# Hybrid encoder layer with expert-choice MoE: merging and routing put in one block, gated sums kept in PSUM, first up weights split earlier, top-k searched on half-length rows, first gather issued by the routing block

## The chip, the cores and the metric

One Trainium2 chip, one core. The time is device microseconds of one launch of the kernel. Three runs of the kernel before gave a median of 2004.21 us (2004.15 to 2004.9).

## The reference, cut to what matters

Two sequences (512 and 256 tokens) get 16 meta tokens in front, so that there are 528 and 272 rows, 800 together, of width 1024. One layer does a mixer (window attention and a long convolution, each gated) and then an expert-choice mixture of 16 experts:

```python
merged = sigmoid(g_a) * (a_out @ w_attn_up) + sigmoid(g_h) * (h_out @ w_hyena_up)
h = h + merged @ w_out
hn = rmsnorm(h)                                   # gain norm_ffn_g
aff = softmax(hn @ w_router)                      # over 16 experts
g, idx = top_k(aff.T, cap)                        # per sequence: 66 of 528, 34 of 272
ye = (silu(hn[idx] @ w_gate[e]) * (hn[idx] @ w_up[e])) @ w_down[e] * g
out = h with ye added at the rows idx, then the final rmsnorm
```

## The kernel before, in words

All matmuls with weights are done in three passes (`three_passes`, lines 242 to 246): both operands are split in a high part, rounded to a narrower format, and a low part, the rest; hi by hi, hi by lo and lo by hi are summed in PSUM. So each weight tile is copied by ScalarE (`..._hi`) and subtracted by VectorE or GpSimd (`..._lo`) before TensorE can use it.

The program is a row of stages. Each is a block with one program per engine, written out by hand, and `end_stage()` behind it clears the stage's semaphores and holds all engines at a barrier.

* `stage_mix`: input projection, attention.
* `stage_hyena` (line 1021 on): the long convolutions by Fourier matmuls. 16 turns (8 pieces of width by 2 orders) go through spectrum (`kf`), forward transform (`zt`, `fwd`), product with the spectrum (`mul` on VectorE, `comb` on GpSimd), turning (`yt`, `yhi` on ScalarE, `ylo` on VectorE) and the way back (`inv`, `gate`). `steps` sets the order on all engines. After the last spectrum matmul SyncE loads the first three up weights and the attention rows (lines 1493, 1495, 1173), stores the last convolution rows (`store_out`, line 1143), and waits until these stores have landed (line 1177).
* `stage_merge` (line 1523 on): 8 weight pieces of 256 columns, each `[128, 4, 256]`; even ones of `w_attn_up`, odd ones of `w_hyena_up`. ScalarE splits the 8 row tiles (`up_in_hi`, line 1557) and the weights (`wu_hi`, line 1554), VectorE makes `up_in_lo` (line 1583), GpSimd `wu_lo` (line 1608). For a pair of pieces TensorE fills 8 PSUM banks: 4 units (two column tiles m, two halves of the 800 rows) by 2 (attention, convolution). VectorE multiplies both by their gates into `gated_pair` (line 1593), adds them into `merged` (line 1599), ScalarE copies that to `merged_hi` (line 1571), VectorE subtracts for `merged_lo` (line 1601). There are 16 units in all. `w_out` is loaded meanwhile, but not split.
* `stage_route` (line 1677 on): ScalarE makes `wo_hi` (line 1784), VectorE and GpSimd `wo_lo` (lines 1814, 1773), by turns. Then seven token tiles: TensorE does `product(i, 0)` and `product(i, 1)` (24 matmuls each), VectorE adds the residual (line 1820), ScalarE squares, a row scale is made, VectorE writes the normalised row `ffn_normed` (line 1827), TensorE turns it (line 1735), both copy it to `ffn_turned`, and TensorE multiplies by the router (line 1746). Then softmax, a transpose of the affinities, and on VectorE the top-k: nine rounds of MAX8, FIND_INDEX8 and MATCH_REPLACE8 (lines 1852 to 1857) on rows of 528, one partition for each expert and sequence. The lists are transposed to slots (`slot_tok`, lines 1866 to 1869). Meanwhile the first expert weights are loaded into the six-deep `w_ring`, and GpSimd splits four halves of them (`we_lo`, line 1777).
* `stage_experts` (line 1997 on): the first gather of rows by GpSimd (line 2000), after a copy of `slot_tok`, and then 16 experts of 12 weight chunks (2 MB each).

Where the order is by hand, a wait on one engine holds everything written behind it on that engine.

## Time and profile before

| what | us |
|---|---|
| median of three runs | 2004.21 |
| the profiled execution, its own time | 2004.04 |
| its span | 2002.2 |
| last row of the convolutions gated | 648.90 |
| first matmul of merging | 656.23 |
| last matmul of merging ends, about | 730.95 |
| first matmul of `product(0, 0)` | 744.95 |
| search of the top values, from and to | 853.75, 872.95 |
| first gather issued | 876.79 |
| first expert matmul | 884.76 |

Busy shares over the whole span: TensorE 93%, VectorE 71%, ScalarE 60%, GpSimd 17%. These are means over stages with different limits, so stages are read one by one below. In the rows, a time is the start in us from the span's start, the next number is the duration, and `[0.56 <-POOL wu_lo L1608]` is the idle time of the engine before the row and what ended it. PE is TensorE, DVE VectorE, ACT ScalarE, POOL GpSimd, SPq SyncE issuing DMAs.

### The profile page before, as it was taken

The numbers are of one execution on the slowest core, as the hardware profiler recorded it, in microseconds if no ns is written. First come the engines' busy times: TensorE is split into PE (matmuls) and PEld (weight loads), VectorE is DVE, ScalarE is ACT, GpSimd is POOL, SyncE is SP. The second block draws the span as 40 slices with busy tenths as digits, with TensorE's granted clock in tenths as the row PEclk, the third lists the DMA queues.
The fourth block names the chain that finished last, engine by engine and source line by source line (L and its number), as shares of the span: only waits on it lengthen the run. The fifth ranks groups of instructions, "written<-read, shape, count | busy, mean of one in ns | idle before, by whom it ended". The sixth has DMA issues, their size and how long they took to land.

```text
span 2002.2 us, 25117 instructions
## 1 busy us (share of the span) xinstructions
PE 1859.7 (93%) x9286; PEld 1449.9 (72%) x9286; DVE 1424.9 (71%) x1431; ACT 1200.3 (60%) x1323; POOL 333.2 (17%) x220
## 2 busy tenths in 40 slices
PE   5999999969998869839999999999999999999996
PEld 5989777848887868627777777777777777777774
DVE  4564211127665662369999999999999999999996
ACT  4225665634433321237777777777777777777776
POOL 1224111135542230040110000011001100010010
PEclk9999999979999889969999999999999999999998
DMA  5332121155012734269999999999999999999994
GB/s 186 105 86 81 54 86 65 40 159 135 23 50 82 254 121 179 103 215 369 361 373 393 376 375 379 388 377 371 383 381 380 372 390 371 374 379 388 377 355 184
DMA packets 239240, 506.51 MB, mean 253 GB/s; under 512 B 20929, under 2 KB 55593, under 8 KB 239112
## 3 DMA queue, kind: packets, MB, share of 16 engines
q1 hardware_dynamic: 228488, 484.63, 66.8%
q0 software_dynamic: 10688, 21.03, 4.4%
q8 instruction: 39, 0.64, 0.1%
q14 instruction: 25, 0.20, 0.0%
HBM read 474.64 MB, written 31.41 MB: 253 GB/s over the span
## 4 chain that ended last, share of the span: by engine, by line
PE 54%; DVE 0%; ACT 0%; issue 0%; DMA 0%; POOL 0%; POOLq 0%; DVEq 0%; ACTq 0%
PE bank L244 18%; PE bank L246 18%; PE bank L245 18%; PE bank L2032 2%; DMA gathered<-ffn_rows,slots_next 0%; ACT we_hi L2090 0%; DVE we_lo L2165 0%; POOL out L2023 0%; DVE w_ring L2246 0%; ACT L2106 0%; DVE expert_out L2230 0%; DVE w_ring L2251 0%; ACT w_ring L2150 0%; DVE hidden L2187 0%; DVE gate_silu L2183 0%
## 5 line engine op out<-in xcount | busy, mean ns | idle before, releaser
L2165 DVE TENSOR_TENSOR we_lo<-w_ring,we_hi 128x2048 fp32r<-128x2048 f32 x380 | 860.6, 2288 | 78.0 <-ACT we_hi L2090 73.3
L2090 ACT ACTIVATE we_hi<-w_ring 128x2048 fp32r<-128x2048 f32 x380 | 724.4, 1914 | 97.6 <-PE bank L246 97.4
L244 PE MATMUL bank<-we_hi,gathered_turned_hi 128*100 128x512 f32 x1024 | 406.9, 397 | 1.4 <-DVE gathered_turned_lo L2169 1.4
L246 PE MATMUL bank<-we_hi,gathered_turned_lo 128*100 128x512 f32 x1024 | 403.2, 394 | 0.0
L245 PE MATMUL bank<-we_lo,gathered_turned_hi 128*100 128x512 f32 x1024 | 402.5, 393 | 0.0
L246 PEld LDWEIGHTS bank<-we_hi,gathered_turned_lo 128*100 128x100 f32 x1024 | 168.5, 165 | 69.6
L244 PEld LDWEIGHTS bank<-we_hi,gathered_turned_hi 128*100 128x100 f32 x1024 | 168.8, 165 | 65.7 <-issue 1.7
L245 PEld LDWEIGHTS bank<-we_lo,gathered_turned_hi 128*100 128x100 f32 x1024 | 168.5, 165 | 65.2
L244 PE MATMUL bank<-normed_hi,w_hi 128*128 128x400 f32 x544 | 199.3, 366 | 11.4 <-ACT gate_sig L635 6.9
L244 PE MATMUL bank<-we_hi,hidden_turned_hi 128*100 128x512 f32 x512 | 204.2, 399 | 0.0
L245 PE MATMUL bank<-we_lo,hidden_turned_hi 128*100 128x512 f32 x512 | 201.6, 394 | 0.0
L246 PE MATMUL bank<-we_hi,hidden_turned_lo 128*100 128x512 f32 x512 | 201.3, 393 | 0.0
L245 PE MATMUL bank<-normed_lo,w_hi 128*128 128x400 f32 x544 | 190.2, 350 | 0.0
L246 PE MATMUL bank<-normed_hi,w_lo 128*128 128x400 f32 x544 | 190.0, 349 | 0.0
L2010 POOL DMA_INDIRECT residual_rows<-expert_out,slots_now x15 | 42.1, 2808 | 840.9 <-DVE expert_out L2199 840.9
L244 PEld LDWEIGHTS bank<-normed_hi,w_hi 128*128 128x128 f32 x544 | 104.8, 193 | 32.5 <-issue 18.2
L852 POOL TENSOR_TENSOR w_lo<-w_raw,w_hi 128x2048 fp32r<-128x2048 f32 x17 | 79.0, 4649 | 273.3 <-ACT w_hi L595 273.3
L246 PEld LDWEIGHTS bank<-we_hi,hidden_turned_lo 128*100 128x100 f32 x512 | 84.3, 165 | 34.0
L244 PEld LDWEIGHTS bank<-we_hi,hidden_turned_hi 128*100 128x100 f32 x512 | 84.4, 165 | 31.3
L245 PEld LDWEIGHTS bank<-we_lo,hidden_turned_hi 128*100 128x100 f32 x512 | 84.5, 165 | 31.0
L245 PEld LDWEIGHTS bank<-normed_lo,w_hi 128*128 128x128 f32 x544 | 104.6, 192 | 0.1
L246 PEld LDWEIGHTS bank<-normed_hi,w_lo 128*128 128x128 f32 x544 | 104.4, 192 | 0.1
(296 smaller groups left out, 2619.3 us busy)
## 6 DMA issues: line engine op xcount, KB each, us to landing
w_ring<-in_w_exp_gate SPq DMA_DIRECT2D x64, 2048.0 KB, 14.0
w_ring<-in_w_exp_up SPq DMA_DIRECT2D x64, 2048.0 KB, 13.7
w_ring<-in_w_exp_down SPq DMA_DIRECT2D x64, 2048.0 KB, 15.5
w_raw<-in_w_in SPq DMA_DIRECT2D x68, 256.0 KB, 4.2
gate_rows<-gate_sig SPq DMA_DIRECT2D x16, 400.0 KB, 2.5
sig_pair<-gate_rows SPq DMA_DIRECT2D x8, 800.0 KB, 5.0
hy_conv_rows<-u_conv SPq DMA_DIRECT2D x12, 400.5 KB, 3.1
w_out<-in_w_out SPq DMA_DIRECT2D x8, 512.0 KB, 7.6
```

Source lines behind the costliest of these rows:

```text
L244: nc.tensor.matmul(out, whi, xhi, start=first, stop=False)
L245: nc.tensor.matmul(out, whi, xlo, start=False, stop=False)
L246: return nc.tensor.matmul(out, wlo, xhi, start=False, stop=last)
L852: nc.gpsimd.tensor_tensor(wlo[c % 2][:, :, :], raw[c % 3][:, :, :], whi[c % 2][:, :, :].bitcast(F32), ALU.subtract).then_inc(w_lo, 1)
L2010: pool.indirect_dma_start(g.accS[:, :], bass.IndirectOffsetOnAxis(ap=cur[0:SLOTS, 0:1], axis=0), ye[0:SLOTS, :], None, compute_op=ALU.add) ...
L2032: last = nc.tensor.transpose(tb[n % 2][:, k * P:k * P + SLOTS], src, ident[0:SLOTS, 0:SLOTS])
L2090: act.activation(whi[(2 * k + half) % 4][:, :], ring[k % RING][:, half * HC:(half + 1) * HC], ACT.Copy).then_inc(w_hi, 1)
L2165: nc.vector.tensor_tensor(wlo[u][:, :], ring[k % RING][:, half * HC:(half + 1) * HC], whi[u][:, :].bitcast(F32), ALU.subtract).then_inc(w_ ...
```

## The change

* `stage_merge` is gone; its work is the first part of `stage_route`, in the same block, with no barrier between.
* Up weights 0 and 1 are split at the end of the convolution block: `wu_hi` on ScalarE behind the last `zhi` step, `wu_lo` on GpSimd at its end. `wu_lo` now lies over the raw weights (in place), so the load of piece i waits until TensorE is done with piece i - 4.
* SyncE's wait for the last stores is moved from the end of the convolution block to the start of the next one.
* For the first pair of pieces TensorE goes by row tile k first and unit second; before it went unit by unit.
* The gated sum stays in the PSUM bank of the convolution half; `merged` and the second half of `gated_pair` are gone. The convolution matmuls of the next pair wait for `m_lo`.
* `w_out` is split during merging: `wo_hi` on ScalarE behind sums 5 to 12, all of `wo_lo` on GpSimd between the up weights.
* TensorE turns the residual row itself, not the normalised one: the gain is multiplied into the router weights (`wrg`, eight more small loads for `gcol`), the row scale into the logits. Sums of squares are taken by halves.
* The top-k rows are halved: the long sequence of each expert lies in two partitions (256 and 272 entries), the short one in a third. Slot j takes the larger of the first list's j-th and the second list's (65 - j)-th.
* GpSimd issues the first gather in the routing block, straight from `slot_tok`. GpSimd's four `we_lo` go to VectorE: two behind `slot_tok`, two in the expert block. One chunk less is loaded ahead.

```diff
@@ stage_hyena, GpSimd, at its end
+            for i in range(2):
+                pool.wait_ge(g.wu_hi_done, i + 1)
+                nc.gpsimd.tensor_tensor(g.wu_lo[i][:, :, :], g.up_w[i][:, :, :], g.wu_hi[i][:, :, :].bitcast(F32), ALU.subtract)\
+                  .then_inc(g.wu_lo_done, 1)
@@ stage_hyena, SyncE, at its end
-            for k in range(4):
-                sp.wait_ge(store[k], 32)
@@ stage_hyena, ScalarE
+                if st == ("zhi", len(TURNS) - 1):
+                    act.wait_ge(kmm, before[len(TURNS)])
+                    for i in range(2):
+                        act.wait_ge(g.up_w_in[i], 32 if i % 2 == 0 else 16)
+                        act.activation(g.wu_hi[i][:, :, :], g.up_w[i][:, :, :], ACT.Copy).then_inc(g.wu_hi_done, 1)
@@ merging, VectorE, one unit
-                    for q in range(2):
-                        last = nc.vector.tensor_tensor(ga[:, q, :], banks[u % 4][q][:, 0:HALF], sig[m % 2][:, q, h * HALF:(h + 1) * HALF],
-                                                       ALU.mult)
-                    last.then_inc(gd, 1)
+                    nc.vector.tensor_tensor(ga[:, :], part[0], gate[0], ALU.mult)
+                    nc.vector.tensor_tensor(part[1], part[1], gate[1], ALU.mult).then_inc(gd, 1)
                     dve.wait_ge(gd, u + 1)
-                    nc.vector.tensor_tensor(mm_[:, :], ga[:, 0, :], ga[:, 1, :], ALU.add).then_inc(summed, 1)
+                    nc.vector.tensor_tensor(part[1], part[1], ga[:, :], ALU.add).then_inc(summed, 1)
@@ merging, ScalarE
+                    if 2 <= m < 6:
+                        out_weights(2 * (m - 2) + b)
@@ merging, TensorE
+                order = [(k, u) for k in range(GROUP) for u in range(4)] if c == 0 else [(k, u) for u in range(4) for k in range(GROUP)]
+                for k, u in order:
+                    if c and k == 0:
+                        pe.wait_ge(m_lo if q else gd, 4 * (c - 1) + u + 1)
@@ routing, TensorE
+                if i < 2 and b == 0:
+                    pe.wait_ge(m_lo, 2 * KT - 3 + i)
...
                     if i == 0 and b == 0:
-                        pe.wait_ge(w_lo[k % 2], k // 2 + 1)
+                        pe.wait_ge(o_lo, k + 1)
+                        pe.wait_ge(m_lo, 2 * k + 1)
...
-                pe.wait_ge(hnd, i + 1)
...
+                    if k % 4 == 0:
+                        pe.wait_ge(h2d, 2 * i + k // 4 + 1)
+                    last = nc.tensor.transpose(g.ps[4 + k // 4][:, (k % 4) * P:(k % 4) * P + m], h[i % 2][0:m, k * P:(k + 1) * P],
                                                ident[0:m, 0:m])
@@ routing, GpSimd
+            pool.wait_ge(slots, 2)
...
+            nc.gpsimd.indirect_dma_start(g.xe[0:SLOTS, :], None, g.hnS[:, :], bass.IndirectOffsetOnAxis(ap=g.slot_tok[0:SLOTS, 0:1], axis=0))\
+              .then_inc(g.gath, 16)
@@ routing, VectorE, at its end
+            for u in range(2):
+                dve.wait_ge(g.ew_hi_done, u + 1)
+                nc.vector.tensor_tensor(g.ew_lo[u][:, :], g.ring[u // 2][:, u % 2 * HC:(u % 2 + 1) * HC], g.ew_hi[u][:, :].bitcast(F32),
+                                        ALU.subtract).then_inc(g.ew_lo_done, 1)
```

Three places where the order on an engine moves. First ScalarE (ACT) at the end of the convolution block. `y_turned` is the turned spectrum that the last two ways back need. Before:

```order
L1344 ACTIVATE z_turned_hi_3802<-bank 128x256
L1346 ACTIVATE z_turned_rest_3774<-bank 16x128
L1347 ACTIVATE z_turned_rest_3774<-bank 16x128
L1358 ACTIVATE y_turned_hi_3811<-bank 128x512
L1364 ACTIVATE y_turned_rest_3813<-bank 32x128
L1365 ACTIVATE y_turned_rest_3813<-bank 32x128
L1358 ACTIVATE y_turned_hi_3811<-bank 128x512
```

and now:

```order
L1347 ACTIVATE z_turned_hi_3809<-bank 128x256
L1349 ACTIVATE z_turned_rest_3781<-bank 16x128
L1350 ACTIVATE z_turned_rest_3781<-bank 16x128
L1373 ACTIVATE wu_hi_3748<-up_weights_3740 128x1024
L1373 ACTIVATE wu_hi_3749<-up_weights_3741 128x1024
L1361 ACTIVATE y_turned_hi_3818<-bank 128x512
L1367 ACTIVATE y_turned_rest_3820<-bank 32x128
```

The two copies, and the waits for their loads, stand ahead of the turning of the last two turns.

Second TensorE (PE) between merging and routing. Before, two branches and the barrier stand between the last up matmul and the first of `product(0, 0)`:

```order
L244 MATMUL bank<-up_in_hi_6986,wu_hi_6989 128x400
L245 MATMUL bank<-up_in_lo_6987,wu_hi_6989 128x400
L246 MATMUL bank<-up_in_hi_6986,wu_lo_6991 128x400
L1523 UNCONDITIONAL_BRANCH
L1714 UNCONDITIONAL_BRANCH
L244 MATMUL bank<-wo_hi_7740,merged_hi_6984 128x512
```

and now:

```order
L244 MATMUL bank<-up_in_hi_6998,wu_hi_3749 128x400
L245 MATMUL bank<-up_in_lo_6999,wu_hi_3749 128x400
L246 MATMUL bank<-up_in_hi_6998,wu_lo_3747 128x400
L244 MATMUL bank<-wo_hi_7004,merged_hi_6996 128x512
L245 MATMUL bank<-wo_lo_7000,merged_hi_6996 128x512
```

The products follow at once.

Third GpSimd (POOL) from merging to the first gather. Before:

```order
L1608 TENSOR_TENSOR wu_lo_6991<-up_weights_3743,wu_hi_6989 128x1024
L1523 UNCONDITIONAL_BRANCH
L226 ISA
L1769 UNCONDITIONAL_BRANCH
L1773 TENSOR_TENSOR wo_lo_7741<-w_out_3739,wo_hi_7740 128x1024 x4
L1777 TENSOR_TENSOR we_lo_3754<-w_ring_66_3744,we_hi_3750 128x2048
```

and now:

```order
L1814 TENSOR_TENSOR wu_lo_3746<-up_weights_3742,wu_hi_3748 128x1024
L1819 TENSOR_TENSOR wo_lo_7000<-w_out_3739,wo_hi_7004 128x1024 x2
L1814 TENSOR_TENSOR wu_lo_3747<-up_weights_3743,wu_hi_3749 128x1024
L1819 TENSOR_TENSOR wo_lo_7000<-w_out_3739,wo_hi_7004 128x1024 x2
L1826 DMA gathered_3764<-ffn_rows,slot_tokens_52 100x1024
```

All eight `wo_lo` are on GpSimd now, within merging, no `we_lo` is, and the gather stands in this block.

## Rows read from the trace of the kernel before

**Rows 1.** Windows: us; busy us (instructions) of PE, PEld, DVE, ACT, POOL; granted clock; DMA share; GB/s
```profile
685.40:703.70 18.30, 17.74 (x97) 17.44 (x97) 10.22 (x16) 4.05 (x6) 4.79 (x2) 1.00 0.48 164
730.95:744.95 14.00, 0.00 (x0) 0.00 (x0) 11.02 (x14) 8.75 (x10) 7.47 (x3) 0.68 0.47 153
744.95:758.69 13.74, 13.74 (x50) 11.03 (x51) 5.87 (x2) 0.00 (x0) 4.79 (x2) 0.82 0.79 292
853.75:872.95 19.20, 0.00 (x0) 0.00 (x0) 18.61 (x43) 3.12 (x2) 15.81 (x4) 0.50 0.98 356
872.95:884.76 11.81, 2.00 (x11) 1.54 (x11) 2.79 (x21) 1.01 (x2) 1.09 (x1) 0.50 0.45 160
884.76:2002.20 1117.44, 1099.99 (x4984) 788.95 (x4984) 1019.69 (x700) 846.04 (x594) 83.91 (x33) 0.99 1.00 363
```

**Rows 2.** Timeline of ACT and DVE at the end of the convolutions
```profile
637.14 0.60 ACT L1358 ACTIVATE y_turned_hi<-bank 128x512 fp32r<-128x512 f32 x1 [2.66 <-PE bank L1276]
...
648.46 0.44 DVE L1466 TENSOR_TENSOR x_short<-bank,x_short 128x272 f32<-128x272 f32 x1 [3.49 <-PE bank L1291]
```

**Rows 3.** SyncE's issue of up weight 1; DMA issues (count, KB, us to landing), weights 0, 1
```profile
634.59 0.61 SPq L1495 DMA_DIRECT2D up_weights<-in_w_hyena_up  x1
...
up_weights<-in_w_attn_up SPq DMA_DIRECT2D x2, 256.0 KB, 4.1
...
up_weights<-in_w_hyena_up SPq DMA_DIRECT2D x1, 512.0 KB, 5.3
```

**Rows 4.** SyncE's wait for the last store; timeline of ACT, PE where merging starts
```profile
SPq L1177 <- DMA mixer_rows<-x_short: 1.3, 1, 1.3
...
651.88 0.87 ACT L1557 ACTIVATE up_in_hi<-attention_rows 128x800 fp32r<-128x800 f32 x1 [7.93 <-PEq L227]
...
659.83 0.87 ACT L1557 ACTIVATE up_in_hi<-hyena_rows 128x800 fp32r<-128x800 f32 x1 [3.85 <-DMA hyena_rows<-mixer_rows]
...
656.23 0.67 PE L244 MATMUL bank<-up_in_hi,wu_hi 128*128 128x400 f32 x1 [7.88 <-POOL wu_lo L1608]
```

**Rows 5.** Timeline of DVE and PE within merging
```profile
673.53 2.24 DVE L1599 TENSOR_TENSOR merged<-gated_pair 128x400 f32<-128x400 f32 x1
...
676.88 1.05 DVE L1593 TENSOR_TENSOR gated_pair<-bank,sig_pair 128x400 f32<-128x400 f32 x2
677.96 0.58 DVE L1599 TENSOR_TENSOR merged<-gated_pair 128x400 f32<-128x400 f32 x1
...
679.63 1.05 DVE L1593 TENSOR_TENSOR gated_pair<-bank,sig_pair 128x400 f32<-128x400 f32 x2
...
685.41 0.42 PE L244 MATMUL bank<-up_in_hi,wu_hi 128*128 128x400 f32 x1 [0.56 <-POOL wu_lo L1608]
```

**Rows 6.** Timeline of PE and DVE in routing: last tile, copies, first search
```profile
846.02 1.06 PE L1735 MATMUL bank<-ident,ffn_normed 32*128 32x32 f32 x8 [4.54 <-DVE ffn_normed L1827]
...
852.51 0.68 DVE L1846 COPY affinity<-bank 16x512 f32<-16x512 f32 x1 [1.74 <-PE bank L1762]
...
853.28 0.43 DVE L1848 COPY affinity<-bank 16x272 f32<-16x272 f32 x1
853.75 0.70 DVE L1852 MAX8 top_values<-affinity 48x8 f32<-48x528 f32 x1
```

**Rows 7.** Timeline of DVE, POOL: slot list, gathers; of the chain: first gather's landing
```profile
874.69 0.15 DVE L1869 TENSOR_TENSOR slot_tokens<-bank,second_group_slots 100x1 uint32<-100x1 f32 x1
...
876.79 1.09 POOL L2000 DMA_INDIRECT gathered<-ffn_rows,slots_next  x1 [7.23 <-DVE slots_next L2261]
...
876.79 4.95 DMA gathered<-ffn_rows,slots_next
...
1039.09 4.49 DVE L2165 TENSOR_TENSOR we_lo<-w_ring,we_hi 128x2048 fp32r<-128x2048 f32 x2 [0.29 <-ACT we_hi L2090]
...
1039.21 3.08 POOL L2000 DMA_INDIRECT gathered<-ffn_rows,slots_next  x1 [8.26 <-DMA residual_rows<-expert_out,slots_now]
...
1176.24 1.03 POOL L2000 DMA_INDIRECT gathered<-ffn_rows,slots_next  x1 [8.19 <-DMA residual_rows<-expert_out,slots_now]
```

More of the change, by code:

```diff
@@ L947, in stage_hyena @@
         S("hy_x2_long0 hy_x2_long1 hy_x2_short0 hy_x2_short1")
-    store = S("hy_store0 hy_store1 hy_store2 hy_store3")
+    store = g.hy_store
     steps = hyena_steps()
@@ L1506, in stage_merge @@
     ulo = sb("up_in_lo", [P, KT, T], F32R)
-    sb.at = g.merge_rest_at
-    whi = [sb("wu_hi", [P, GROUP, WCH], F32R) for _ in range(2)]
-    wlo = [sb("wu_lo", [P, GROUP, WCH], F32R) for _ in range(2)]
+    sb.at = g.up_rows_at
+    olo = sb("wo_lo", [P, KT, D], F32R)
+    whi, wlo = g.wu_hi, g.wu_lo
+    sb.at = g.merge_rest_at + 2 * GROUP * WCH * 4
     sig = [sb("sig_pair", [P, 2, T]) for _ in range(2)]
-    ga = sb("gated_pair", [P, 2, HALF])
-    mm_ = sb("merged", [P, HALF])
-    (up_in, u_hi, u_lo, wh, wl, sg0, sg1, prod, gd, summed, m_hi, m_lo) = S(
-        "mg_up_in mg_u_hi mg_u_lo mg_wh mg_wl mg_sg0 mg_sg1 mg_prod mg_gated mg_sum mg_m_hi mg_m_lo")
@@ L1515, in stage_merge @@
-    sgs = [sg0, sg1]
+    ga = sb("gated", [P, HALF])
+    sb.at = g.merge_rest_at + 2 * GROUP * WCH * 4 + 4 * T * 4 + 3 * HALF * 4
+    ohi = sb("wo_hi", [P, KT, D], F32R)
+    assert sb.at <= nc.sbuf_usable_end, sb.at
+    sb.at = g.merge_rest_at - 4 * GROUP * WCH * 4
+    h = [sb("residual_in", [P, D]) for _ in range(2)]
+    hn = [sb("ffn_normed", [P, D]) for _ in range(2)]
+    gain = sb("ffn_gain", [P, D])
+    hT = sb("ffn_turned", [P, KT, P])
+    wr = sb("w_router", [P, KT, E])
+    wrg = sb("w_router_gain", [P, KT, E])
@@ new lines, in stage_route @@
+    gcol = sb("ffn_gain_col", [P, KT])
+    ss = sb("square_sums", [P, 3, NTOK])
+    rs = sb("row_scale", [P, NTOK])
+    lg = sb("logits", [P, NTOK, E])
+    red = sb("softmax_cols", [P, 2, NTOK])
+    EE = 64 + E
+    ROWS = (slice(0, E), slice(32, 32 + E), slice(64, EE))
+    PART = 2 * P
+    WIDE = LENS[0] - PART
+    parts = sb("affinity_by_token", [P, NTOK, EE])
+    af = [sb(f"affinity{x}", [EE, WIDE]) for x in range(2)]
+    rounds = -(-CAPS[0] // 8)
+    val = sb("top_values", [EE, 8 * rounds])
@@ L1516, in stage_merge, with row_parts @@
+    hin, st, hst, sgs = [hin0, hin1], [st0, st1], [hst0, hst1], [sg0, sg1]
+    pieces = [token_pieces(t0, m, io["x_prompt"][0], io["x_sample"][0], io["meta_tokens"]) for t0, m in TOK_TILES]
+    total = [[0, 0]]
+    for i, ps_ in enumerate(pieces):
+        now = list(total[-1])
+        now[i % 2] += 16 * len(ps_)
+        total.append(now)
     banks = [(g.ps[0], g.ps[1]), (g.ps[2], g.ps[3]), (g.ps[4], g.ps[5]), (g.ps[6], g.ps[7])]
-    NW = 2 * NCH
+    acc = banks[0:2]
     def up(k):
         return g.up_attn[:, k, :] if k < GROUP else g.up_hyena[:, k - GROUP, :]
+    def row_parts(k):
+        return [slice(0, HALF), slice(HALF, T)] if k == 0 else [slice(0, T)]
@@ L1529, in load_sig, with load @@
                 sp.dma_start(sig[m % 2][:, :, :], g.sigS.rearrange("(q m p) t -> m p q t", q=2, p=P)[m]).then_inc(sgs[m % 2], 16)
+            def load(i):
+                if i >= 2:
+                    sp.wait_ge(trn, i - 1)
+                    sp.wait_ge(hnd, i - 1)
+                    sp.wait_ge(hst[i % 2], 16 * (i // 2))
+                for r0, src in pieces[i]:
+                    sp.dma_start(h[i % 2][r0:r0 + src.shape[0], :], src).then_inc(hin[i % 2], 16)
+            for k in range(4):
+                sp.wait_ge(g.hy_store[k], 32)
             for k in range(GROUP, KT):
@@ L1686, in _ @@
+                    load_sig(2)
+                    load_sig(3)
+            for m in range(4, KT):
+                load_sig(m)
+            sp.wait_ge(upd, 4 * NW)
             load(0)
@@ L1874 @@
 RING = 6
-AHEAD = RING + 2
+AHEAD = RING + 1
 FCH = FE // 4
@@ L1915, in stage_experts @@
     ye = sb("expert_out", [P, D])
+    gain = sb("final_gain", [P, D])
+    first_rows = sb("first_rows", [P, D])
+    assert sb.at <= g.ew_lo_at, sb.at
+    sb.at = g.ex_small
     nxt = sb("slots_next", [P, 1], U32)
@@ L1926, in stage_experts @@
     row_of = [sb("out_row", [P, 1], U32) for _ in range(2)]
-    gain = sb("final_gain", [P, D])
-    first_rows = sb("first_rows", [P, D])
+    assert sb.at <= g.up_rows_at, sb.at
     def ring_part(k, i):
@@ L2269, in _ @@
                 turn_lo(c, "x", c)
+            for half in range(2):
+                lo_of(0, 1, half)
             nc.vector.memset(stat[:, :], 1.0).then_inc(fconst, 1)
```

493 lines of the change are left out of this document (237 added, 256 removed).

## The prediction

> **What bounds the kernel now.** I read the busy shares first, then the windows by stage, then the timelines at the seams, then the waits. The experts take 1117.44 us of the span [rows 1], and TensorE works in 1099.99 of them at granted clock 0.99, so nothing on VectorE, ScalarE or the queues has a price there as long as it keeps its lead. The change touches the 236 us between the end of the convolutions (648.90, the end of the gate in [rows 2]) and the first expert matmul (884.76). There TensorE is the bound within the stages: between 685.40 and 703.70 it works 17.74 of 18.30 us [rows 1]. What can be had lies at the seams, where it stands still: 656.23 - 648.90 = 7.3 us ahead of merging, 14.00 us between merging and routing [rows 1], and the tail from the last tile's turning (846.02 [rows 6]) to 884.76, a chain of short work on VectorE, 19.20 us of it the search [rows 1]. The measurement can tell about 0.2% from no change, 4 us.
>
> **The sum, part by part,** against the profiled execution's own 2004.04 us, which lies 0.17 under the median.
>
> *1. The two weight copies on ScalarE, +3.9.* They stand ahead of the turning of the last two turns, and wait for their loads. Weight 0 was issued just before 634.59 and took 4.1 us, weight 1 was issued at 634.59 and took 5.3 [rows 3]: it is there at 639.9. A copy of 512 columns takes 0.60 us [rows 2], of 800 0.87 [rows 4], so one of 1024 some 1.05. So ScalarE is free at 640.95, where it began `y_turned_hi` at 637.14 [rows 2], waiting only for TensorE: +3.8, and 0.1 for TensorE's clock, which may fall meanwhile. Queued behind it are the copies for the last two ways back; VectorE's low part and, behind that in its order, the last product with the spectrum wait too, then GpSimd's sum and TensorE's turning. Nothing of this chain has slack, so the block ends at 652.8, not 648.9. GpSimd's two `wu_lo` come behind its own last work and end before that. Bounds: 0 if the loads land 4 us sooner, +9 if they take 10 us.
>
> *2. The stores' wait, -1.4.* SyncE waited 1.3 us [rows 4] before the barrier could open; ScalarE began merging at 651.88 [rows 4], 3.0 us behind the gate. Now the queue's issue of the store and the barrier are left, some 1.6. The loads of the convolution rows still wait for the stores, so they move by the 3.9 less about 1: `hyena_rows` let ScalarE go on at 659.83 [rows 4], now at 662.6.
>
> *3. First up matmul, -3.2.* It came at 656.23, 4.35 us behind ScalarE's start, held by `wu_lo` [rows 4]. Now the weights are ready, and it waits for half a row tile on ScalarE and VectorE: 1.15 us. It starts at 655.4. By row tiles first, each tile gives TensorE 12 matmuls, 2.2 us or more, where VectorE needs 1.0; the first attention half lasts to 666.3, and the late convolution rows are split by 664.6. That cover is 1.7 us: if it goes, the late rows are paid one by one.
>
> *4. Within merging, -0.9.* Before, TensorE waited for `wu_lo` once a pair, 0.56 us idle [rows 5] and 0.7 with the slower restart, three times: 2.1. In the steady pairs this goes, since piece i is split a half pair earlier. But in the first pair all four units now end together, while VectorE takes 2.75 us for one (679.63 - 676.88 [rows 5]); the second pair waits for the gates of its third and fourth unit, 0.6 each: 1.2. The convolution half's wait for `m_lo` falls 6 us behind its need. A unit costs TensorE 4.4 us, so VectorE's 2.75 stay covered. That the sum of 2.24 us beside a GpSimd instruction goes [rows 5], 0.58 otherwise, saves nothing: it was covered. GpSimd takes 4.79 us for two `wu_lo` [rows 1], so six of them and eight `wo_lo` of the same size some 34 us in 60; ScalarE's eight copies fit too, and both are done before they are needed.
>
> *5. The seam, -14.0.* `product(0, 0)` needs the sum of its last tile only at its last k, 4.9 us in, and VectorE is 4.6 behind. All 14.00 us [rows 1] go. The first pair then comes without the spell of low clock: its 13.74 us at 0.82 [rows 1] are 11.27 at full, *-2.5*. The small loads (`gcol`) land about as the first product ends, and the turning that needs them is a product later: 0.
>
> *6. Last tile to the search, -1.8.* The last turning waited 4.54 us for the normalised row [rows 6]. Now it waits for the residual alone, but ScalarE's copy for the router matmul still stands behind its squares and root: I take 2.1 of the 4.54, less 0.3 for a clearing that the exponential waits for and for affinities in three pieces. Ends: 0 and -3.7.
>
> *7. Copies, search, lists, -6.15.* A VectorE copy costs (0.68 - 0.43) / 240 = 1.04 ns a column [rows 6]. 26 instructions (nine MAX8, nine FIND_INDEX8, eight MATCH_REPLACE8, 0.7 us each) shorten by 256 columns: 26 x 0.267 = -6.9, of 19.20. Copies shared with ScalarE: -0.35. Two more list pieces and a choice of five small instructions more: +1.1. Ends of the search: -5.5 if the fixed part weighs more, -7.5.
>
> *8. The gather, +0.2.* From the slot list (874.84 [rows 7]) to the gather's issue at 876.79 is 1.95 us, and it lands 4.95 later [rows 7], so 6.9. Now it is issued without the copy and the barrier, 0.7 behind the list. But VectorE starts `we_lo` at once. At 1039.21 a gather issued 0.12 us into a `we_lo` took 3.08 us, ending 0.9 behind the first of the two (4.49 / 2); at 1176.24 one took 1.03 [rows 7]. I take the former: it ends 3.25 us behind the list, lands 3.86 after that, 7.1: +0.2. The barrier, behind VectorE's 4.6 us, opens at 5.7 and is covered. If it isn't held: -1.0.
>
> The Trainium skill's page "SBUF — State Buffer" (section "Who interferes with whom") speaks against the value I take. It says that a `tensor_tensor` with both inputs in SBUF contends only with GpSimd's reads, and infers that writing descriptors isn't held by it. By that rule the gather goes ahead, the barrier becomes the later one, and the sum is about 1.2 us lower; the row of 3.08 us disagrees.
>
> *9. The experts, 0.* VectorE has two halves more to split, 4.5 us [rows 7], just behind the first turned rows; chunk 1 is needed one chunk later, 5.8 us (1117.44 / 192) or more at the low clock. One chunk less is loaded ahead; chunk 7 is issued some 5 us into the experts and needed five chunks in, at 29. The engine that bounds this stage does the same work.
>
> Sum: 3.9 - 1.4 - 3.2 - 0.9 - 14.0 - 2.5 - 1.8 - 6.15 + 0.2 = -25.85, so 1978.2 us, 1.3% less. **Forecast: 1978.**
>
> **The rivals.**
> *A. The seam stays in part.* GpSimd is late with `wo_lo`: its eight wait for ScalarE's copies, these for the sums, and then each row tile of the first product is paced by 2.4 us or more, not 0.7. For: before, four of them took GpSimd 7.47 + 4.79 us beside VectorE [rows 1]. Against: VectorE's instructions in merging now read at most one SBUF operand, and the last sum that a copy waits for is the twelfth of 16. If four were left, 10 us come back: 1988.
> *B. ScalarE's stall is dear.* The loads take 10 us instead of 5: +5, 1983. For: the four attention rows, 1.6 MB, are issued right behind them. Against: they were before too, when the rows of 4.1 and 5.3 us were taken [rows 3].
> *C. Slower than before.* The mechanism: PSUM as source and target of VectorE's gate and sum. If each of these two instructions costs what the sum cost when it was blocked, 2.24 instead of 0.58 [rows 5], a unit takes 2.75 + 2 x 1.67 = 6.1 us, over TensorE's 4.4. From 4.4 on it decides, 16 units by 1.7 us are 27, and the time is 2005 to 2009. Against: no row here reads or writes PSUM on VectorE at such a price; the gates already read it, at 0.53 each.
> *D. The waits are replaced and nothing moves*: the tail's gain is lost to the gather, and the seam's to `m_lo`. 2000 to 2006. I see no row for it.
>
> **Chances.** Forecast with its unknown costs (1972 to 1984): 0.80. A: 0.06. B: 0.08. C: 0.03. D: 0.03. What is under 1972 lies in the first. The unknown costs: part 1 from -3.9 to +5 against my value, part 6 from -1.9 to +1.8, part 7 from -0.6 to +1.4, part 8 -1.2, an earlier return of the clock at the start -2, stalls in merging up to +3. Not all fall on one side; I reach from 1971 to 1985. Faster by over 0.2% (under 2000) in the forecast, A and B, and a little of D: 0.95. Within: 0.02. Slower: 0.03.
>
> **What would show it.** In the new profile: ScalarE idle some 5 us ahead of `wu_hi`, released by the up weights' load, and the last gate near 652.8; TensorE's first up matmul near 655.4; one or two waits of 0.6 us at the second pair and none later; `product(0, 0)` right behind the last up matmul, near 728 to 729; FIND_INDEX8 at 0.43; the gather of 3 us on GpSimd from the slot list on, and the first expert matmul near 859; then 1117 us of experts. The prediction falls if TensorE stands still between merging and routing, if a unit on VectorE takes over 4.4 us, or if the experts' stretch is longer by more than 2 us.

## The result, and the profile after

The changed kernel took 1984.04 us in the median of four runs (1982.3 to 1984.68), the kernel before 2004.18 on the same chip: a ratio of 0.9906, 95% interval 0.9893 to 0.9919. So it is 0.9% faster, 20 us, where the forecast said 26 and 1978. 0.9906 of 2004.21 is 1985.4, just outside the range that ended at 1985; the median itself, 1984.04, is at its edge. The profiled execution took 1984.68 us, its span 1982.9.

Read in the forecast's own order. First the windows by stage of the changed kernel (us; busy us (instructions) of PE, PEld, DVE, ACT, POOL; granted clock; DMA share; GB/s): merging, first product pair, search, slot list to first expert matmul, experts.

```profile
656.18:729.22 73.04, 72.37 (x385) 71.31 (x386) 37.74 (x66) 25.79 (x35) 33.36 (x14) 0.98 0.59 206
729.22:740.30 11.08, 11.08 (x49) 9.01 (x49) 5.49 (x13) 1.01 (x2) 0.00 (x0) 1.00 0.66 183
832.84:845.19 12.35, 0.00 (x0) 0.00 (x0) 11.77 (x43) 6.87 (x4) 0.00 (x0) 0.50 1.04 389
848.43:866.14 17.71, 1.57 (x8) 1.29 (x9) 5.92 (x9) 1.01 (x2) 5.04 (x1) 0.50 0.47 142
866.14:1982.90 1116.76, 1099.04 (x4984) 788.41 (x4984) 1023.78 (x705) 846.04 (x594) 75.97 (x33) 0.99 1.00 365
```

They answer to [rows 1]. The granted clock is a share of full speed. The stop of 14.00 us between merging and routing is gone: merging ends and routing begins within one row, and the first pair runs at full clock in 11.08 us instead of 13.74. The search fell from 19.20 to 12.35. The experts are as long as before, 1116.76 for 1117.44. One window went the other way: from slot list to first expert matmul it was 884.76 - 874.84 = 9.92 us, and is 17.71.

ScalarE at the end of the convolutions, timeline, beside [rows 2]:

```profile
639.39 1.06 ACT L1373 ACTIVATE wu_hi<-up_weights 128x1024 fp32r<-128x1024 f32 x1 [3.63 <-DMA up_weights<-in_w_attn_up]
641.33 1.06 ACT L1373 ACTIVATE wu_hi<-up_weights 128x1024 fp32r<-128x1024 f32 x1 [0.88 <-DMA up_weights<-in_w_hyena_up]
642.29 0.58 ACT L1361 ACTIVATE y_turned_hi<-bank 128x512 fp32r<-128x512 f32 x1
...
648.86 0.60 ACT L1361 ACTIVATE y_turned_hi<-bank 128x512 fp32r<-128x512 f32 x1 [5.56 <-PE bank L1279]
...
654.89 3.24 ACT L1655 ACTIVATE up_in_hi<-attention_rows 128x400 fp32r<-128x400 f32 x5 [5.02 <-PEq L227]
```

Both copies wait for their loads, and `y_turned_hi` stands behind them. TensorE in merging and at the seam, timeline, beside [rows 4, 5]:

```profile
656.18 0.67 PE L244 MATMUL bank<-up_in_hi,wu_hi 128*128 128x400 f32 x1 [3.31 <-DVE up_in_lo L1707]
...
680.53 0.45 PE L244 MATMUL bank<-up_in_hi,wu_hi 128*128 128x400 f32 x1 [0.28 <-DVE bank L1719]
683.26 0.45 PE L244 MATMUL bank<-up_in_hi,wu_hi 128*128 128x400 f32 x1 [0.26 <-DVE bank L1719]
...
729.03 0.34 PE L246 MATMUL bank<-up_in_hi,wu_lo 128*128 128x400 f32 x1
729.22 0.39 PE L244 MATMUL bank<-wo_hi,merged_hi 128*128 128x512 f32 x1
```

TensorE waits three times in all. The last row is `product(0, 0)`, directly behind the last up matmul. VectorE beside it, one unit with PSUM as source and target:

```profile
676.69 0.56 DVE L1718 TENSOR_TENSOR gated<-bank,sig_pair 128x400 f32<-128x400 f32 x1
677.17 0.57 DVE L1719 TENSOR_TENSOR bank<-bank,sig_pair 128x400 f32<-128x400 f32 x1
677.77 0.58 DVE L1721 TENSOR_TENSOR bank<-bank,gated 128x400 f32<-128x400 f32 x1
678.93 0.58 DVE L1723 TENSOR_TENSOR merged_lo<-bank,merged_hi 128x400 fp32r<-128x400 f32 x1 [0.57 <-ACT merged_hi L1674]
679.42 0.56 DVE L1718 TENSOR_TENSOR gated<-bank,sig_pair 128x400 f32<-128x400 f32 x1
```

A unit takes 679.42 - 676.69 = 2.73 us. The place that decided, all engines' timelines from the slot list on, beside [rows 7]:

```profile
848.28 0.15 DVE L1804 TENSOR_TENSOR slot_tokens<-pick 100x1 uint32<-100x1 f32 x1
848.34 4.49 DVE L1807 TENSOR_TENSOR we_lo<-w_ring,we_hi 128x2048 fp32r<-128x2048 f32 x2
848.75 5.04 POOL L1826 DMA_INDIRECT gathered<-ffn_rows,slot_tokens  x1 [126.53 <-DVE slot_tokens L1804]
852.86 0.37 SPq L1933 DMA_DIRECT2D w_ring<-in_w_exp_gate  x1
863.20 1.57 PE L2074 MATMUL bank<-ident,gathered 100*128 100x100 f32 x8 [16.17 <-PEq L227]
866.14 0.74 PE L244 MATMUL bank<-we_hi,gathered_turned_hi 128*100 128x512 f32 x1 [1.38 <-DVE gathered_turned_lo L2211]
```

The DMA issues of that stretch (us from issue to landing), and the block's last instruction on GpSimd's queue (duration ns min/median/max, first and last start):

```profile
w_ring<-in_w_exp_gate SPq DMA_DIRECT2D x1, 2048.0 KB, 10.5
gathered<-ffn_rows,slot_tokens POOLq DMA_INDIRECT x1, 13.4
```

```profile
L1581 POOLq DRAIN  x1: 13767/13767/13767, 848.5 to 848.5; - x1
```

The 17.71 us are now a plain sum. GpSimd begins 0.32 us behind the slot list. The issue takes 5.04 us and ends at 853.79, 0.96 behind the second `we_lo` (848.34 + 4.49 = 852.83). Weight chunk 6, 2 MB, is issued at 852.86, 0.9 us ahead of that end, and the gather's data land at 848.75 + 13.4 = 862.15. GpSimd's drain, the end of its block, lasts to 862.27, so the barrier opens only behind the landing and TensorE turns the first rows at 863.20. 0.32 + 13.4 + 1.05 + 2.94 = 17.71.

### The profile page after: what moved, and what is told of

Read it like the earlier page. It is cut to its first block, busy times and chain, and to the rows that moved or that the text cites. A ratio compares the mean times of both kernels' runs of the same rounds, so it can differ in the third digit from the quotient of the medians.

```text
span 1982.9 us, 25130 instructions
## 1 busy us (share of the span) xinstructions
PE 1855.6 (94%) x9286; PEld 1445.9 (73%) x9286; DVE 1409.5 (71%) x1447; ACT 1202.1 (61%) x1340; POOL 318.1 (16%) x220
## 4 chain that ended last, share of the span: by engine, by line
PE 54%; DVE 1%; issue 0%; ACT 0%; POOL 0%; POOLq 0%; DVEq 0%; ACTq 0%
PE bank L245 18%; PE bank L244 17%; PE bank L246 17%; PE bank L2074 2%; DVE we_lo L2207 1%; DVE w_ring L2272 0%; ACT we_hi L2132 0%; POOL out L2065 0%; DVE w_ring L2288 0%; ACT L2148 0%; DVE expert_out L2272 0%; DVE w_ring L2293 0%; ACT w_ring L2192 0%; DVE gate_silu L2225 0%; ACT gate_sigmoid L2148 0%
## 6 DMA issues: line engine op xcount, KB each, us to landing
w_ring<-in_w_exp_up SPq DMA_DIRECT2D x64, 2048.0 KB, 14.7
```

## The experiments

The profiled executions differ by some us ahead of anything that the change touches: ScalarE's last copy of the spectra begins at 633.03 before, at 634.31 after, and between 628.95 and 633.95 in the runs below. So "from the spectra" counts from there: before, the last gate ends after 15.87 us, the first up matmul comes after 23.20, the first product after 111.92, the search after 220.72, and the slot list is done after 241.81. "List to expert" is from the slot list's end to the first expert matmul. Ratios are against the kernel before on the same chip, with 95% intervals; they are 2.6 to 3.8 us wide to either side of the value, so smaller differences of the kernel's time are not told apart by them. The stretches of one profile each agree far better where the code is the same (MAX8 to the slot list: 15.58 to 15.60 us in every profile with the narrow search), so the parts are read from stretches.

**The changed kernel once more**, on another chip.

> The changed kernel itself, unaltered, on the same chip as the kernels beside it, as their measure. Expected: 1984 within 1.5 us; from ScalarE's last copy of the spectra to the last gate of the convolutions 19.1 to 20.1 us, to the first up matmul 21.9 to 22.8, from the slot list's end to the first expert matmul 17.7.

Measured: 1986.9 us, 0.9919 (0.9903 to 0.9935). Last gate after 20.04, first up matmul 22.80, first product 96.71, search 200.37, slot list 215.96; list to expert 17.51. The stretches agree with the first profile within 1.9 us, and the one at the gather within 0.2.

**What the loss at the gather consists of.** The first edit takes chunk 6 out of the routing block:

```diff
-AHEAD = RING + 1
+AHEAD = RING
```

> Only the seventh weight chunk's load is taken out of the routing block (it is issued first thing in the experts). Theory: the 17.7 us from slot list to first expert matmul are GpSimd's issue held by VectorE's two low parts (5.0 us), then the gather's data behind the 2 MB chunk, then GpSimd's drain until it has landed. Without the chunk ahead the gather lands some 4 to 5 us behind the issue's end instead of 8.4, and the first expert matmul comes 3.5 to 4.5 us sooner: about 1980. Rival 1, the chunk is no matter and the hold alone delays: no change, 1984. Rival 2, the block's end itself (drain, clearing, barrier) is long whatever the gather does: no change, and the drain does not end with the landing. If the chunk is late in the experts instead, the experts' stretch of 1116.8 us grows by what was won.

Measured: 1981.91 us, 0.9887 (0.987 to 0.9903). List to expert 13.55 us, 4.2 less than 17.71. The issue was held just as long, the landing came sooner, and the drain shrank with it (timeline of GpSimd; DMA issues; GpSimd's drain):

```profile
850.15 5.05 POOL L1826 DMA_INDIRECT gathered<-ffn_rows,slot_tokens  x1 [126.55 <-DVE slot_tokens L1804]
```

```profile
gathered<-ffn_rows,slot_tokens POOLq DMA_INDIRECT x1, 9.2
```

```profile
L1581 POOLq DRAIN  x1: 9598/9598/9598, 849.9 to 849.9; - x1
```

So the 2 MB ahead of the gather's data cost it 4.2 us, and both rivals fall: the chunk does matter, and the block's end is long only because of the gather. The experts took 1117.93 us, for 1116.76 and 1118.73 in the two profiles of the changed kernel; the later chunk cost nothing that can be seen.

The second moves the two low parts to GpSimd, ahead of the slot list. That is where they stood before the change, with two more, four in the time of a search of 19.20 us:

```diff
         def _(pool):
+            for u in range(2):
+                pool.wait_ge(g.ew_hi_done, u + 1)
+                nc.gpsimd.tensor_tensor(g.ew_lo[u]...)        # taken out of VectorE's program
             pool.wait_ge(slots, 2)
```

> The two low parts of the first expert weights are moved from VectorE, behind the slot list, to GpSimd, ahead of it in the time of the search. Theory: GpSimd's issue of the gather is then not held (1.0 to 1.1 us instead of 5.0), and chunk 6, whose load waits for the low parts, has landed before: the gather lands 4 to 5 us behind its issue, the drain ends with it, and the first expert matmul comes some 9.5 us behind the slot list instead of 17.7: 8 us less, about 1976. Rival 1 (block end long by itself): under 1 us less. Rival 2 (GpSimd beside the search slows VectorE): the search of 12.35 us grows by up to 2 us, and 6 us are left of the 8.

Measured: 1975.34 us, 0.9853 (0.9837 to 0.987). List to expert 10.01 us, 7.7 less. GpSimd's timeline, the DMA issues, the drain:

```profile
829.77 9.09 POOL L1818 TENSOR_TENSOR we_lo<-w_ring,we_hi 128x2048 fp32r<-128x2048 f32 x2 [112.19 <-ACT we_hi L1700]
844.13 1.09 POOL L1826 DMA_INDIRECT gathered<-ffn_rows,slot_tokens  x1 [5.27 <-DVE slot_tokens L1804]
```

```profile
gathered<-ffn_rows,slot_tokens POOLq DMA_INDIRECT x1, 5.7
```

```profile
L1581 POOLq DRAIN  x1: 6057/6057/6057, 843.9 to 843.9; - x1
```

The issue takes 1.09 us, the data land 5.7 behind its start, and MAX8 to the slot list takes 15.59 us as in the changed kernel, with GpSimd's 9.09 us beside it: both rivals fall. Hold (5.04 - 1.09 = 3.95) and chunk (4.2) make 8.15, and 7.7 came back: the data landed 4.6 us behind the issue's end, where it was 4.15 in the kernel without chunk 6. The experts took 1120.46 us in this profile, the longest of all sixteen (the others 1115.7 to 1118.7), so this profile alone doesn't show that the whole gain is kept; the three kernels further down with the same edit took 1115.7 to 1118.1 there.

**What holds the issue.** In two kernels the subtractions are replaced by instructions of another kind on the same tiles, so that the first chunk's low part is left out (lines shortened):

```diff
-                nc.vector.tensor_tensor(g.ew_lo[u], ring_half, g.ew_hi[u], ALU.subtract)
+                nc.vector.tensor_copy(g.ew_lo[u], ring_half)                          # one kernel
+                nc.vector.tensor_reduce(g.ew_lo[u], ring_half.unsqueeze(2), AX.X, ALU.max)   # the other
```

> VectorE's two low parts behind the slot list are replaced by copies of the weights (one input from SBUF instead of two); this leaves out the subtraction for the first chunk's low part. Theory: GpSimd's issue of the gather is held because VectorE reads two inputs from SBUF; with one input it is not held, and takes 1.0 to 1.1 us instead of 5.0, although VectorE is busy. Rival 1, any long VectorE instruction on SBUF holds it: it ends some 0.9 us behind the end of the first or second copy. Rival 2, the hold is not VectorE's but the queue's or the stores': 5 us as before.

> VectorE's two low parts behind the slot list are replaced by reductions over an axis of one element, which read one input from SBUF and run at one element a cycle; this leaves out the subtraction for the first chunk's low part. Theory: GpSimd's issue is not held by VectorE being busy as such, but by instructions that take the port the two share; the reduction does not, so the issue takes 1.0 to 1.1 us while VectorE works for 4 us beside it. Rival, every long VectorE instruction on SBUF holds it: the issue ends some 0.96 us behind the end of the first or second reduction.

Timelines of VectorE and GpSimd, first with copies:

```profile
847.35 2.35 DVE L1807 CAST we_lo<-w_ring 128x2048 fp32r<-128x2048 f32 x2
847.75 2.91 POOL L1825 DMA_INDIRECT gathered<-ffn_rows,slot_tokens  x1 [126.56 <-DVE slot_tokens L1804]
```

then with reductions:

```profile
846.84 4.47 DVE L1807 TENSOR_REDUCE we_lo<-w_ring 128x2048 fp32r<-128x2048 f32 x2
847.24 1.09 POOL L1825 DMA_INDIRECT gathered<-ffn_rows,slot_tokens  x1 [126.58 <-DVE slot_tokens L1804]
```

With the copies (1981.34 us in one run, list to expert 15.99) the issue ends at 850.66, 0.96 behind the second copy; my theory, that it takes two inputs from SBUF, falls, and its rival 1 came true. With reductions it takes 1.09 us inside 4.47 us of VectorE work, so it isn't VectorE's being busy either, and that rival falls as well. What holds it is a kind of instruction: subtractions with two inputs in SBUF and copies (2048 columns in 1.2 us, against 2.2 for either of the others). The gather then went ahead of chunk 6, landed after 5.2 us, and list to expert was 9.49 us (1974.44 in one run) with nothing moved to GpSimd.

Why to the end of the second? One low part of the two is moved:

```diff
-            for u in range(2):        # VectorE, behind the slot list
+            for u in range(1, 2):     # u = 0 is on GpSimd, ahead of the slot list
```

> The first of the two low parts is on GpSimd ahead of the gather, the second stays on VectorE behind the slot list. Theory: the issue is held while VectorE's low parts follow one another without a gap, to the end of the last: with one left it ends 0.96 us behind that one, some 2.8 us after its start instead of 5.04, and the first expert matmul comes about 2.2 us sooner behind the slot list, 15.5 us. Rival, the issue needs several turns of the port and takes one between the two: it would then take about as long, 3 us, but end at another place than 0.96 behind the low part.

Measured: 1978.1 us (one run); list to expert 15.45. VectorE and GpSimd:

```profile
844.28 2.29 DVE L1807 TENSOR_TENSOR we_lo<-w_ring,we_hi 128x2048 fp32r<-128x2048 f32 x1
844.68 2.84 POOL L1830 DMA_INDIRECT gathered<-ffn_rows,slot_tokens  x1 [9.71 <-DVE slot_tokens L1804]
```

The issue ends 0.95 us behind the one low part, where the theory put it. In seven profiles with two subtractions it ended 0.96 behind the second (and so with the two copies). But this is no rule, as the expert loop shows, where low parts also come in pairs without a gap. Of the 224 gathers there from `ffn_rows` (16 profiles), 150 began 0.055 us or more behind the start of a low part, and each ended 0.90 to 0.92 us behind the end of that same one, with the next instruction already under way. The other 74, begun at most 0.04 us behind its start, or ahead of it, took 1.03 us. Only the last gather of each profile, from `residual_rows`, was held to the end of the second, in all 16; in the kernel before (timelines of VectorE and GpSimd):

```profile
1929.29 4.48 DVE L2165 TENSOR_TENSOR we_lo<-w_ring,we_hi 128x2048 fp32r<-128x2048 f32 x2
1930.58 4.09 POOL L2000 DMA_INDIRECT gathered<-residual_rows,slots_next  x1 [8.46 <-DMA residual_rows<-expert_out,slots_now]
```

Why some gathers get in behind the first of two and others only behind the second was not tried. Chunk 6 was still ahead of it, issued at 846.59, and the gather landed 11.1 us behind its start.

**The gather back behind the barrier.**

```diff
         def _(pool):            # expert block
+            nc.gpsimd.indirect_dma_start(g.xe..., g.hnS..., slot_tok[0:SLOTS, 0:1])   # taken out of routing
             for e in range(E - 1):
```

> The first gather is issued behind the barrier again (from the slot list itself, without the copy of before); everything else as in the changed kernel, so VectorE's low parts and chunk 6 stay where they are. Theory: the barrier opens behind the low parts, some 1.1 us after 852.8, the issue takes 1.1 us, and chunk 6 is still ahead of the data, so the gather lands at about the same time as now (862 to 863.5); what goes is the drain and the barrier behind the landing, 1.0 us. First expert matmul 0 to 1 us sooner: 1983 to 1984. Rival, issuing in routing is worth what it was meant to be: 1 to 2 us slower than the changed kernel, 1985 to 1986. Rival, the drain costs much more than 1 us: 3 us or more less.

Measured: 1984.47 us, 0.9906 (0.989 to 0.9923): the changed kernel's ratio. List to expert 17.22 us. GpSimd's drain, then its timeline and TensorE's:

```profile
L1581 POOLq DRAIN  x1: 45/45/45, 847.6 to 847.6; - x1
```

```profile
854.25 1.09 POOL L2044 DMA_INDIRECT gathered<-ffn_rows,slot_tokens  x1 [133.14 <-issue]
861.59 1.60 PE L2074 MATMUL bank<-ident,gathered 100*128 100x100 f32 x8 [15.64 <-DMA gathered<-ffn_rows,slot_tokens]
```

Without a gather in flight the drain takes 45 ns. TensorE starts as soon as the rows are there, not 1.05 us later. Issuing it 6.6 us sooner, as the changed kernel does, made the first expert matmul 0.3 to 0.5 us later. Neither rival came true.

**The copies of the first up weights last on ScalarE.**

```diff
-                if st == ("zhi", len(TURNS) - 1):
+                if st == ("yhi", len(TURNS) - 1):
                     ...                               # the two wu_hi
```

> ScalarE's two copies of the first up weights stand behind its last turned rows in the long convolutions instead of ahead of the rows before. Theory (part 1 of the sum): the copies and the wait for their loads held the chain at the end of the convolutions by 3.9 us with the clock; that goes, and GpSimd's low parts end at about the block's end or 0.6 us behind: 3.0 to 3.9 us less, about 1980.5. Rival, the chain had slack or the clock's fall sets it: under 1 us less. Rival, the low part comes too late for the first up matmul: it waits for wu_lo again, and 1 us or less is left.

Measured: 1983.27 us, 0.9895 (0.9878 to 0.9911), which alone tells nothing. The stretches do: the last gate comes after 15.87 us, the very figure of before, where ten kernels with the copies ahead show 19.04 to 20.74, in the mean 19.8. ScalarE and GpSimd:

```profile
643.37 0.60 ACT L1361 ACTIVATE y_turned_hi<-bank 128x512 fp32r<-128x512 f32 x1 [4.77 <-PE bank L1279]
...
644.42 2.01 ACT L1373 ACTIVATE wu_hi<-up_weights 128x1024 fp32r<-128x1024 f32 x2
```

```profile
645.55 4.69 POOL L1104 TENSOR_TENSOR wu_lo<-up_weights,wu_hi 128x1024 fp32r<-128x1024 f32 x2 [1.89 <-ACT wu_hi L1373]
```

The first rival falls. Of the 3.9 us, 1.1 go to the wait for GpSimd's second low part (to 650.24, behind the gate's end at 649.34), and the first up matmul comes after 19.77 instead of 22.5 (mean of the ten): 2.8 us less.

**The first up weights split behind the barrier again.**

```diff
-        ...                           # the two wu_hi and two wu_lo in the convolutions' block
         act.wait_ge(g.up_attn_in, 16 * GROUP)
-        for k in range(GROUP):
+        weights(0)
+        rows(0)
+        weights(1)
+        for k in range(1, GROUP):
             rows(k)
...
-        for i in range(2, NW):        # GpSimd's wu_lo
+        for i in range(NW):
```

> The first two up weights are copied and split behind the barrier again, as in the kernel before, all else as in the changed kernel. Theory (parts 1 and 3 of the sum): the last gate comes 3.7 us sooner, 15.9 behind the last spectra, as in the kernel before, but the first up matmul waits for ScalarE's 1.05 and GpSimd's 2.4 us, 3.5 us or more, and ScalarE's rows and the second piece come later: about the same time as the changed kernel, within 1.5 us. Rival A, splitting in the convolutions is dear: 2 us or more less. Rival B, it pays: 3 us or more slower.

Measured: 1985.46 us, 0.9918 (0.9899 to 0.9936), against 0.9919 of the changed kernel beside it. Last gate after 15.88, first up matmul 21.47; but TensorE then waited for a row tile once more (waits of TensorE, us in total, times, longest), and the first product came after 96.85, where the nine kernels with the copies ahead and no wait at the seam have 94.91 to 97.05:

```profile
PE bank L244 <- DVE up_in_lo L1701: 7.4, 2, 6.1
```

So splitting these weights in the convolutions is worth nothing that can be seen where it was placed: what part 3 wins, part 1 costs.

**A wait at the seam.**

```diff
+            pe.wait_ge(m_lo, 2 * KT)
             product(0, 0)
```

> TensorE waits for VectorE's last low part of the gated sums before the first product of routing, as a barrier between merging and routing would make it; all else as in the changed kernel. Theory (part 5 of the sum): what the one block gives is this overlap. VectorE's last gate comes behind TensorE's last up matmul and its low part some 3 us after, so TensorE stands still for 3 to 4.5 us, and with the clock's fall behind it the first product comes that much later: 1987 to 1990, 3 to 5 us slower than the changed kernel. Rival, the 14 us of before were the barrier and the loads behind it and not VectorE's lead: under 1 us slower.

Measured: 1993.55 us, 0.9948 (0.993 to 0.9967). The wait, from the same view, and the windows behind it:

```profile
PE bank L244 <- DVE merged_lo L1723: 4.6, 1, 4.6
```

From the first product to the search it is 106.12 us instead of 103.65. So a stop of 4.6 us costs 7.1. The first of the two windows, right behind the stop, was granted a clock of 0.53 of full, about the lower of the two levels (1.2 and 2.4 GHz), though TensorE is busy all through it; in the next 5 us it is 1.00:

```profile
735.00:740.00 5.00, 5.00 (x14) 3.88 (x13) 1.05 (x5) 0.00 (x0) 0.00 (x0) 0.53 0.74 162
740.00:745.00 5.00, 5.00 (x23) 4.08 (x22) 0.69 (x1) 0.72 (x2) 0.00 (x0) 1.00 1.05 398
```

This puts back 4.6 of the 14.00 us. The barrier itself, and the splitting of `w_out` behind it, were not put back: that they are gone is read from the trace of the changed kernel.

**A wide search.**

```diff
-    af = [sb(f"affinity{x}", [EE, WIDE]) for x in range(2)]
+    af = [sb(f"affinity{x}", [EE, LENS[0]]) for x in range(2)]
```

> The two affinity buffers are 528 columns wide again instead of 272, the added columns hold -1, and the nine rounds of the search read all of them; everything else as in the changed kernel. Theory (part 7 of the sum): 26 instructions by 256 columns by 1.04 ns: the search takes 19.2 us instead of 12.4, and nothing hides it: 6.9 us slower, about 1991 to 1993. Rival, the fixed part of an instruction weighs more and the copies were the gain: 5 us or less.

Measured: 1991.1 us, 0.995 (0.9933 to 0.9967). From the search's start to the slot list 22.53 us instead of 15.59: 6.94, as worked out from 1.04 ns a column; the rival's 5 us or less falls.

**The edits that help, together**: low parts on GpSimd and copies last.

> Both edits at once: the low parts of the first expert weights on GpSimd during the search, and the first up weights' copies behind ScalarE's last turned rows. Theory: the two gains lie on the one chain and add, 7.7 at the gather and 2.5 at the start: 10 us less than the changed kernel, about 1974. Rival: what is won ahead of the experts is given back there, because their weight chunks are not there sooner: then the experts' stretch is longer than 1118 by the difference.

Measured: 1972.56 us, 0.9857 (0.9839 to 0.9874); from the spectra to the first expert matmul 222.00 us, where the changed kernel has 231.83 and 233.47. The two gains add in the stretches (one edit alone has 224.86 or 230.33 there), and the experts took 1118.12, within what the two profiles of the changed kernel have. It is 1.4% below the kernel before. The ratios do not tell it from 0.9853 with the low parts on GpSimd alone, nor from the next two.

**Both, and GpSimd's second low part of the up weights behind the barrier.**

> As both edits at once, and GpSimd's second low part of the up weights goes back behind the barrier. Theory: with the copies last, the block's end waited 1.1 us for GpSimd's second low part; that goes, and the piece is needed 9 us later: 1.1 us less than both edits, about 1973. Rival: GpSimd at the start of merging, beside VectorE's low parts of the rows, holds these (both inputs of both in SBUF), and the first up matmul, a VectorE low part behind ScalarE's start, comes up to 2 us later: 0 to 1 us slower than both edits.

```diff
-            for i in range(2):        # GpSimd's wu_lo, convolutions
+            for i in range(1):
...
-            for i in range(2, NW):    # the same, routing
+            for i in range(1, NW):
```

Measured: 1972.81 us, 0.9855 (0.9839 to 0.9872). The barrier opens sooner (ScalarE starts after 17.36 us, not 18.48), but the first up matmul comes later, after 20.29, not 19.77. VectorE, then GpSimd:

```profile
651.71 5.40 DVE L1707 TENSOR_TENSOR up_in_lo<-attention_rows,up_in_hi 128x400 fp32r<-128x400 f32 x5 [2.05 <-ACT up_in_hi L1655]
```

```profile
651.15 2.35 POOL L1810 TENSOR_TENSOR wu_lo<-up_weights,wu_hi 128x1024 fp32r<-128x1024 f32 x1 [2.90 <-POOLq L227]
```

GpSimd came first, and VectorE's low parts waited for it, 5.40 us for five that take 3.98 in the changed kernel: TensorE's first matmul came 2.93 us behind ScalarE's start instead of 1.29. The rival was right.

**Both, and the first gather behind the barrier again.**

> Both edits at once (the first expert weights' low parts on GpSimd, the up weights' copies last), and the first gather is issued behind the barrier again. Theory: the barrier opens about 1.4 us behind the slot list, the issue takes 1.1, the data 3.9 to 5, the turning and first split 2.9: 9.5 to 10.4 us from the slot list to the first expert matmul, against 10.0 with the gather in the routing block, where the drain takes back what the earlier issue gives: within 1 us of the kernel with both edits, about 1973. Rival, the early issue is worth the barrier and the copy, as meant: 1.5 us or more slower.

Measured: 1973.57 us, 0.9854 (0.9836 to 0.9873); list to expert 10.30 us, against 9.98 with the gather in routing. Even where nothing is in its way, issuing it in the block before is worth 0.3 us (one profile of each).

## Why the prediction was wrong

The sum up to the slot list was right. From the spectra to the slot list's end it was 241.81 us, and is 214.12 to 216.30 in eight profiles, of the changed kernel and of kernels that differ from it only around the gather, in the mean 215.5: 26.3 us less, where parts 1 to 7 gave 26.05. The whole error is step 8.

* *Part 1, the copies on ScalarE, +3.9*: right, mechanism and size. The loads took 4.9 and 5.0 us in the median of this stretch, and the ten profiles against the one with the copies last give 3.9. Rival B (loads of 10 us) did not happen.
* *Parts 2 and 3, to the first up matmul*: from the spectra it was to be 3.9 - 1.4 - 3.2 = 0.7 sooner, and was 23.20 - 22.5 = 0.7. It follows ScalarE's start by 1.29 us (1.15 expected). What I had not asked is whether parts 1 and 3 are worth more together than left alone; they are not.
* *Part 4, within merging, -0.9*: the two waits came at the second pair and none later, at 0.28 and 0.26 us where 0.6 each was expected. From the first up matmul to the first product it was 88.72 us, and is 73.04 to 74.01, 14.7 to 15.7 less, where parts 4 and 5 gave 14.9.
* *Part 5, the seam, -14.0 and the clock's -2.5*: right. The row at 729.22 follows the one at 729.03, the first pair runs in 11.08 us at clock 1.00, and a wait put back there costs 4.6 and 2.5 more. The other 9.4 us of the stop rest on the trace alone.
* *Part 6 and the copies of part 7, -1.8 and -0.35*: from the first product to the search 108.80 us became 103.62 to 103.67, 5.15 less, of which the first pair gave 2.7, so 2.5 for 2.15. No run takes these two parts back by themselves.
* *Part 7, search and lists*: 19.20 to 12.35 is -6.85, for -6.9; the lists and the choice take 15.59 - 12.35 = 3.24 us where it was 1.89 (872.95 to 874.84), so +1.35 for +1.1.
* *Part 8, the gather, +0.2*: **this step failed**; it was +7.8. It said three things. "It ends 3.25 us behind the list": it took the row at 1039.21 for the rule, where the issue ended 0.9 behind the first of the two low parts. That is the frequent case in the loop of the kernel before, 11 of 15 gathers beside low parts; three were not held, and the last, at 1930.58, was held to the end of the second. Here too it ended 0.96 behind the second, 5.36 us behind the list. That is 2.1 us. "Lands 3.86 after that": taken from a gather with nothing ahead of it, while chunk 6 waits for the low parts and so is set free 0.9 us ahead of the held issue's end; 8.36 us instead, so 4.5. I had costed the chunk only where it is needed, in part 9, and not at the queue that it is moved past. "The barrier opens at 5.7 and is covered": it cannot open while GpSimd drains, so it comes behind the landing, 1.05 us. 2.1 + 4.5 + 1.05 = 7.65; the rest is in the turning and rounding.
* *Part 9, the experts, 0*: 1116.76 and 1118.73 in the two profiles of the changed kernel, 1117.44 before.

Of the rivals, A and C fall by the rows: no stop at the seam, and 0.57 and 0.58 us for the instructions that have PSUM as source and target, 2.73 for a unit where 4.4 would decide. Of D the first half came true nearly in full: parts 6 and 7 won 8.0 us, and the gather lost 7.8. I had set it aside because I saw no row for it; the row at 1930.58 would have been one, for 2.1 of the 7.6 us.

The low value (the gather not held, -1.0) was weighed with the Trainium skill, page "SBUF — State Buffer", section "Who interferes with whom". On its rule the rows divide: a reduction leaves the issue at 1.09 us and copies hold it, both as the page says; but it infers that a `tensor_tensor` with both inputs in SBUF does not hold descriptor writing, and the rows of 5.04 and 2.84 us disagree, as do the 150 held gathers of the loop.

## What to carry to other kernels

When a step is moved ahead of a barrier, ask what the barrier waits for afterwards: a transfer started by GpSimd in the block's last microseconds becomes part of the block, because the drain at its end lasts until the data have landed. Ask next which transfers the neighbouring work sets free at that moment, since a small gather behind a 2 MB load pays for the load. And look at what VectorE does while GpSimd writes an indirect transfer's descriptors; three ways out were seen here: the low parts on GpSimd earlier (7.7 us less from list to expert), an instruction kind that doesn't hold it, or one low part in place of two. In the loop, a gather that began no later than 0.04 us behind a low part was not held either.

## What the runs showed that I had not expected

* GpSimd's drain at a block's end takes 45 ns with nothing under way and 13.77, 11.50, 9.60 and 6.06 us with a gather in flight that lands after 13.4, 11.1, 9.2 and 5.7: it ends with the landing.
* The first gather's issue takes 1.09 us beside reductions or nothing, 2.84 with one subtraction (SBUF with SBUF) under way, 5.04 with two and 2.91 with two copies, and ends 0.95 or 0.96 us behind the last of them. In the expert loop, as at 1039.21 [rows 7], the issue ended 0.90 to 0.92 us behind the first of two in 150 of 150 held gathers from `ffn_rows`, and 0.90 or 0.91 behind the second in 16 of 16 from `residual_rows`; the cause of the difference is open.
* Which starts first matters: a GpSimd low part that began 0.56 us ahead held VectorE's (5.40 us for five instead of 3.98), and a gather begun up to 0.04 us behind a low part took 1.03 us, one begun 0.055 us or more behind it 1.27 to 3.14. But two of GpSimd's beside MAX8, FIND_INDEX8 and MATCH_REPLACE8, 9.09 us, left the stretch from search to slot list at 15.59.
